# Reordering the first expert step of a hybrid SSD, Hyena and PEER backbone

## Chip, cores and metric

One core of one Trainium2 chip runs the whole program. The metric is the device time in microseconds from launch to end; lower is better. "Step", "turn" and "expert k" below are the program's own units and are explained with the kernel.

## The reference

A backbone of two layers works on 256 latent tokens of width 1024 (with 256 context tokens that only the first mixer reads). Layer 0 mixes tokens with a bidirectional Mamba-2 scan, layer 1 with an order-2 Hyena operator; after each mixer comes a PEER block. All arithmetic is float32. Per layer:

```python
x = layer_norm(DEEPNORM_ALPHA * x + g1 * y_lat, ln_g[i, 0], ln_b[i, 0])
x = layer_norm(DEEPNORM_ALPHA * x + g2 * peer_ffn(x * (1 + sc2) + sh2, *peer_w), ln_g[i, 1], ln_b[i, 1])
```

and the PEER block, cut to what matters:

```python
q = (t @ wq).reshape(T, PEER_HEADS, PEER_DK)                 # 8 heads, 256 wide
s1 = einsum('thd,hkd->thk', q[..., :half], k1)               # 128 keys per half
s2 = einsum('thd,hkd->thk', q[..., half:], k2)
v1, i1 = top_k(s1, 16); v2, i2 = top_k(s2, 16)
top_s, pos = top_k(v1[..., :, None] + v2[..., None, :], 16)  # 16 experts of 128*128
gate = softmax(top_s)
act = gelu(einsum('td,thkd->thk', t, u_tab[idx]))
out = einsum('thk,thkd->td', gate * act, v_tab[idx])
```

The Hyena filters are `sin` networks of 64 hidden features at 256 lags times a weight `h_f_w3` (64 by 2 orders, 2 sides, 1024 channels), with decay and a norm over the lags, taken to the frequency domain.

## The kernel before

**Tiles and steps.** The 256 tokens are two tiles of 128 (tile 0, tile 1). `peer(l)` runs the PEER block of layer l in 16 steps: step s is head s % 8 of tile s // 8. A step has 16 experts per token, k = 0 to 15, taken two at a time in a turn (`PAIR`). I number the experts of a layer through: expert 0 to 15 are step 0, expert 16 is the first of step 1.

**One expert's way.** POOL issues an indirect DMA (`pool.indirect_dma_start`, L1288) that gathers for each token its expert's two rows, 8 KB to each of 128 partitions, 1 MiB, into one of 8 slots (`uv`). DVE makes the dot product of the first row with the token (L2222), ACT the GELU of the turn's two dots (L1509), DVE multiplies by the gate (`weigh_experts`, L2154), ACT scales an identity to a diagonal (`diagonals`, L1517), and PE multiplies the second row by the diagonal into the output sum (`combine`, L1056), which frees the slot for the gather of the expert 8 later. For layer 0, slots 0 to 5 hold output weights of the mixer first: gather n of the first six waits for `out_weights_used` to reach n + 2, which `mixer_out(1, k0, k1)` counts up once for each second k; gathers 6 and 7 wait for its last product.

**What stands between the experts.** Each engine's order is written out by hand. On DVE, `choose(s, piece)` is the top-k of a later step in 8 pieces (0 to 3 the four top-8 searches of the two halves, 4 the candidate sums, 5 the top 16 of 256, 6 and 7 positions and expert numbers), placed in the turns between the dots and `weigh_experts`. The first step's choice, `choose_first`, stands ahead of all turns, as does `gates_of(0)`, which waits for ACT's `gate_exp(0)`. PE makes the queries of head s + 2 in four chunks of 8 products (`queries`, L1032) and their scores (L1043) in step s; ACT copies both out of PSUM (L1303) between its diagonals, in its own order, so a copy holds back the GELU behind it. Both heads 0 and 1 are handled ahead of the steps for tile 0 (`first_queries` L973, `second_queries` L999, `second_scores` L1009), woven into the mixer's output product of tile 1 (`mixer_out`, L934). Tile 1's own first norm, `second_tile` (`ln_stats`, `ln_norm`, `modulate_tile`: L1988 to L2027 and L1701), is done on DVE inside step 0, with PE's `tile_transposes(0, 1)` (L962) in the middle. The names of the turns in step 0 that place these pieces are the conditions `k == ...` of the listing.

**The filters.** In steps 8 to 15 of layer 0 the Hyena filters are made in four pieces (`filter_products` L1080 on PE, `filter_sides` and others on DVE). SP loads each piece's weights `w3` (`filter_piece`, L703): two DMAs, one for each side, each to 64 partitions, 128 KB each.

```python
w3 = early[0:HY_FF, 0:4, :].rearrange("p (s r) c -> p s r c", s=2)
hidden = dotj[0:HY_FF, 0:T]
```

The functions that the change touches follow.

## Time and profile before

| | |
|---|---|
| median of 3 runs | 1937.98 us (1936.33 to 1944.38) |
| profiled execution, its own time | 1935.79 us |
| its span, first to last instruction | 1934.0 us |
| granted TensorE clock, mean | 0.971 |
| busy: PE, DVE, ACT, POOL | 1690.3, 1500.2, 593.4, 483.3 us |
| HBM read | 662.79 MB, 343 GB/s over the span |
| gathers of expert rows | 512, 536.90 MB |
| layer 0's first gather issued, last part of its steps | 408.19 us, some 1088 us |

A page of the profile gives busy times by engine, the span in 40 slices, the DMA queues, the chain of work that ended last, and the costliest groups. The trace behind it gives each engine's instructions in order of time: start in us from the span's start, length, engine, line, operation, output <- inputs by the program's names, shapes, number merged, and in brackets the idle time ahead and what ended it. PE's rows count each float32 product several times (a `combine` is 4 rows, a k of `mixer_out` is 4).

### The profile page before, as it was taken

What the parts mean: (1) busy time and instruction counts of PE and PEld (TensorE: products, weight loads), DVE (VectorE), ACT (ScalarE), POOL (GpSimd) and SP (SyncE); (2) the same over time, 40 slices, a digit from 0 to 9 for tenths busy, and PEclk for the clock granted to TensorE, in tenths of its full rate; (3) what the DMA queues carried; (4) which work ended last, traced back from release to release, by engine and by line L of the source; (5) the groups of instructions that cost most, each with busy time, mean ns of one, the idle gap of its engine ahead of it and who ended that gap; (6) DMA issues with size and microseconds to landing.
All of it is one profiled execution on the core that took longest, in us unless ns stands there. A gap on an engine that the chain in (4) does not pass through costs nothing.

```text
span 1934.0 us, 18185 instructions
## 1 busy us (share of the span) xinstructions
PE 1690.3 (87%) x5422; PEld 934.6 (48%) x5422; DVE 1500.2 (78%) x3548; ACT 593.4 (31%) x1427; POOL 483.3 (25%) x516
## 2 busy tenths in 40 slices
PE   5999999997999877899898999879989987877776
PEld 5778468653554432343343677545444433332232
DVE  6899996766778767888886699787678778777755
ACT  2555672312222323323242121023222232322221
POOL 0000000022334333343333100023333333333331
PEclk9999999998999998998999999889999999999999
DMA  8333118978999999999999775679999999999996
GB/s 348 120 120 113 50 58 316 387 276 347 364 427 419 426 408 406 380 418 413 425 414 426 312 302 201 245 294 415 427 426 426 421 425 414 417 426 420 426 417 280
DMA packets 95170, 665.11 MB, mean 344 GB/s; under 512 B 11323, under 2 KB 13020, under 8 KB 15456
## 3 DMA queue, kind: packets, MB, share of 16 engines
q0 software_dynamic: 73728, 536.90, 67.3%
q1 hardware_dynamic: 21344, 127.05, 17.0%
q8 instruction: 43, 0.70, 0.1%
q14 instruction: 55, 0.45, 0.1%
HBM read 662.79 MB, written 1.11 MB: 343 GB/s over the span
## 4 chain that ended last, share of the span: by engine, by line
PE 47%; DMA 24%; DVE 20%; issue 4%; ACT 2%; PEld 1%; DVEq 0%; PEldq 0%; POOL 0%; SPq 0%; POOLq 0%; ACTq 0%
DMA expert_rows<-in_p_uv,chosen_experts 23%; PE bank L1056 23%; DVE dot_products L2222 4%; PE bank L1032 4%; PE bank L818 3%; PE bank L862 3%; PE bank L934 2%; DVE conv_work_or_state L1860 2%; DVE silu_c_row_and_products L1668 2%; PE bank L878 1%; PE bank L889 1%; PE bank L1248 1%; PE bank L1092 1%; ACT weight_diagonal L1517 1%; PE bank L1175 1%
## 5 line engine op out<-in xcount | busy, mean ns | idle before, releaser
L1056 PE MATMUL bank<-expert_rows,weight_diagonal 128*128 128x512 f32 x2048 | 967.8, 617 | 173.5 <-ACT weight_diagonal L1517 172.8
L1288 POOL DMA_INDIRECT expert_rows<-in_p_uv,chosen_experts x512 | 483.1, 944 | 1424.3 <-PE bank L1056 795.1
L2222 DVE SCALAR_TENSOR_TENSOR dot_products<-expert_rows,bank 128x1024 f32<-128x1024 f32 x512 | 624.9, 1220 | 255.6 <-DMA expert_rows<-in_p_uv,chosen_experts 241.6
L1056 PEld LDWEIGHTS bank<-expert_rows,weight_diagonal 128*128 128x128 f32 x2048 | 385.2, 196 | 689.1 <-issue 398.0
L1517 ACT ACTIVATE weight_diagonal<-constants,expert_weights 128x128 f32<-128x128 f32 x512 | 177.8, 394 | 243.8 <-DVE expert_weights L2154 235.3
L1509 ACT ACTIVATE expert_gelu<-expert_dots 128x2 f32<-128x2 f32 x258 | 52.3, 203 | 627.4 <-DVE dot_products L2222 627.0
L818 PE MATMUL bank<-mixer_input_T_hi,weights_hi 128*128 128x512 f32 (+1 forms) x192 | 74.8, 389 | 22.0 <-DVE mixer_input_T_lo L1752 14.7
L1860 DVE SCALAR_TENSOR_TENSOR conv_work_or_state<-conv_work_or_state,channel_vectors 128x252 f32<-128x252 f32 (+1 forms) x192 | 82.5, 431 | 4.9 <-ACT conv_work_or_state L1371 0.4
L1175 PE MATMUL bank<-hyena_input_T,hyena_weight_block 128*128 128x256 f32 x320 | 71.1, 380 | 4.3 <-DMA hyena_weight_block<-in_h_in_blocks 4.3
L818 PE MATMUL bank<-mixer_input_T_lo,weights_hi 128*128 128x512 f32 (+1 forms) x192 | 72.4, 377 | 0.0
L818 PE MATMUL bank<-mixer_input_T_hi,weights_lo 128*128 128x512 f32 (+1 forms) x192 | 72.4, 377 | 0.0
L1175 PEld LDWEIGHTS bank<-hyena_input_T,hyena_weight_block 128*128 128x128 f32 x320 | 60.2, 190 | 14.8 <-DMA hyena_weight_block<-in_h_in_blocks 5.6
L2154 DVE TENSOR_TENSOR expert_weights<-expert_gelu,expert_gates 128x2 f32<-128x2 f32 x258 | 41.8, 162 | 30.7 <-ACT expert_gelu L1509 22.8
L1668 DVE SCALAR_TENSOR_TENSOR silu_c_row_and_products<-weight_block,silu_c_row_and_products 128x1024 f32<-128x1024 f32 x48 | 58.6, 1222 | 2.4
L862 PE MATMUL bank<-weight_block,mixer_input_T 128*128 128x256 f32 x256 | 58.5, 382 | 0.0
L1032 PE MATMUL bank<-t_T,weight_block 128*128 128x256 f32 x224 | 53.2, 380 | 0.0
L818 PEld LDWEIGHTS bank<-mixer_input_T_hi,weights_hi 128*128 128x128 f32 x192 | 37.1, 193 | 30.8 <-issue 14.8
L1032 PEld LDWEIGHTS bank<-t_T,weight_block 128*128 128x128 f32 x224 | 42.9, 192 | 18.4 <-issue 14.0
L862 PEld LDWEIGHTS bank<-weight_block,mixer_input_T 128*128 128x128 f32 x256 | 47.6, 190 | 7.5 <-issue 1.6
L1509 ACT ACT_TABLE_LOAD x38 | 48.8, 1283 | 0.7
L934 PE MATMUL bank<-out_weights,output_input_T 128*128 128x512 f32 x96 | 42.2, 592 | 0.0
L2222 DVE DVE_READ_ACCUMULATOR dot_products<-expert_rows,bank 128x1 f32 x512 | 42.2, 82 | 0.0
(298 smaller groups left out, 1935.8 us busy)
## 6 DMA issues: line engine op xcount, KB each, us to landing
weight_block<-in_ada_rows SPq DMA_DIRECT2D x24, 1024.0 KB, 7.0
weight_block<-in_m_in_blocks SPq DMA_DIRECT2D x20, 1024.0 KB, 4.9
hyena_weight_block<-in_ada_rows SPq DMA_DIRECT2D x16, 1024.0 KB, 5.4
hyena_weight_block<-in_h_in_blocks SPq DMA_DIRECT2D x12, 1024.0 KB, 7.3
weight_block<-in_wq_blocks SPq DMA_DIRECT2D x11, 1024.0 KB, 7.6
expert_rows<-in_p_uv,chosen_experts POOLq DMA_INDIRECT x512
out_weights<-in_m_out_blocks SPq DMA_DIRECT2D x6, 1024.0 KB, 9.5
hyena_weight_block<-in_h_out_blocks SPq DMA_DIRECT2D x4, 1024.0 KB, 7.2
```

What stands on the lines that cost most here:

```text
L818: last = mm(ps[b][:, c0:2 * T], lhs[q % 2][:, k, :], rhs[:, k, c0:2 * T], start=(k + n == 0), stop=(k == KD - 1 and n == 2))
L862: last = mm(ps[b][:, t * BLK:(t + 1) * BLK], hT[:, k, T + t * P:T + (t + 1) * P], w[:, k * BLK:(k + 1) * BLK], start=(k == 0), stop=(k == ...
L934: last = mm(ps[b][:, :], uT[:, t, k, :], out_w[k // 2][:, k % 2, h * 512:(h + 1) * 512], start=(k == 0), stop=(k == INNER // P - 1))
L1032: last = mm(ps[b][:, c * T:(c + 1) * T], wk[:, c * P:(c + 1) * P], tT[:, k, :], start=(k == 0), stop=(k == KD - 1))
L1056: last = mm(ps[b][:, :], dg[n % DIAG][:, :], uv[slot][:, D + h * 512:D + (h + 1) * 512], start=(r == 0 and k == 0), stop=end)
L1175: last = mm(ps[b][:, c * T:(c + 1) * T], w[:, k * BLK + c * P:k * BLK + (c + 1) * P], hhT[:, k, :], start=(k == 0), stop=(k == KD - 1))
L1288: pool.indirect_dma_start(uv[slot][:, :], None, A[f"p_uv{l}"], bass.IndirectOffsetOnAxis(ap=chosen[:, s_, k:k + 1], axis=0)).then_inc(uv_l ...
L1509: f(gel[:, s_, k:k + width], dots[:, s_, k:k + width], ACT.Gelu).then_inc(sem("gelu_done"), 1)
L1517: f(dg[n % DIAG][:, :], ident, ACT.Copy, scale=ew[:, s_, k:k + 1]).then_inc(sem("diagonal_ready"), 1)
L1668: stt(dotj[:, :], weights_, 1.0, c_rows[row], ALU.mult, ALU.mult, accum_out=o[:, m // KD, m % KD:m % KD + 1]).then_inc(sem("modulation_row ...
L1860: last = stt(o, s_, conv_tap(q, i, j), o, ALU.mult, ALU.add)
L2222: stt(prod[:, :], uv[slot][:, 0:D], 1.0, rows_t, ALU.mult, ALU.mult, accum_out=dots[:, s_, k + j:k + j + 1]).then_inc(sem("dots_done"), 1)
```

## The change

Six things change, all in layer 0, and five of them ahead of or inside step 0:

- PE ahead of the steps: `token_rows(0, 0)` and three of `mixer_out(1, ...)`'s k (5 to 7) stand ahead of the second head's queries; two more k (8, 9) stand between its queries and its scores, and six behind.
- PE, step 0: tile 1's transposes stand ahead of expert 2 (were ahead of expert 6). Head 2's query chunks come at k = 4, 6, 8, 10 (were 8, 10, 12, 14), its scores at k = 12 (were 15).
- DVE, step 0: `second_tile` follows the turn of experts 2 and 3 (was 4 and 5). The choice for step 1 starts in the first turn: pieces 0, 1; then 2, 3; then 4; then 5; then 6, 7 (were pairs in turns 1 to 4).
- ACT, step 0: `ln_root` at k = 2 (was 4); head 2's queries are copied at k = 10, its scores at k = 12 (both were at 14).
- SP: a filter piece's weights are one DMA of 256 KB to 128 partitions, side 0 on partitions 0 to 63 and side 1 on 64 to 127, from a table that the host lays out in that order; the hidden features are loaded twice (64 KB each), once for each half of the partitions.
- PE's filter products of side 1 then read partitions 64 to 127.

Layer 1's conditions give the same turns as before.

```diff
-    w3 = early[0:HY_FF, 0:4, :].rearrange("p (s r) c -> p s r c", s=2)
+    w3 = early[:, 0:2, :]
...
-    hidden = dotj[0:HY_FF, 0:T]
+    hidden = dotj[:, 0:T]
...
         wait_full(sp, ("q", 0, HALVED))
-        sp.dma_start(hidden, hdram).then_inc(sem("filter_in"), 16)
+        for side in range(2):
+            sp.dma_start(hidden[side * HY_FF:(side + 1) * HY_FF, :], hdram).then_inc(sem("filter_in"), 16)
...
-            c = A["h_f_w3"][0][:, o * 2 * D:(o + 1) * 2 * D].rearrange("p (s c) -> p s c", s=2)
-            for side in range(2):
-                sp.dma_start(w3[:, side, :, :], halves(c[:, side, h * 512:(h + 1) * 512])).then_inc(sem("filter_weights_in"), 16)
+            sp.dma_start(w3, halves(A["filter_weights"][m])).then_inc(sem("filter_weights_in"), 16)
...
-                        pe.wait_ge(sem("filter_weights_in"), 32 * (m + 1))
-                        pe.wait_ge(sem("filter_in"), 32)
+                        pe.wait_ge(sem("filter_weights_in"), 16 * (m + 1))
+                        pe.wait_ge(sem("filter_in"), 48)
                     for side in range(2):
                         b = begin(("hflt", m, t, side))
-                        mm(ps[b][:, :], hidden[:, t * P:(t + 1) * P], w3[:, side, :, :], start=True, stop=True).then_inc(full[b], 1)
+                        f = slice(side * HY_FF, (side + 1) * HY_FF)
+                        mm(ps[b][:, :], hidden[f, t * P:(t + 1) * P], w3[f, :, :], start=True, stop=True).then_inc(full[b], 1)
...
-                    if l == 0 and s_ == 0 and k == 6:
+                    if l == 0 and s_ == 0 and k == 2:
                         tile_transposes(0, 1)
...
-                    chunks = ((8, 10, 12, 14), (2, 5, 8, 11))[l] if s_ == 0 else (0, 1, 2, 3)
+                    chunks = ((4, 6, 8, 10), (2, 5, 8, 11))[l] if s_ == 0 else (0, 1, 2, 3)
...
-                    if r < PH and k == min(chunks[-1] + 2, TOPK - 1):
+                    if r < PH and k == chunks[-1] + 2:
                         scores(r)
...
         first_half_scores(0, 1)
+        token_rows(0, 0)
+        mixer_out(1, 5, 8)
         for c in range(2):
             second_queries(0, 0, c, 0, KD)
-        mixer_out(1, 5, 6)
+        mixer_out(1, 8, 10)
         second_scores(0, 0)
-        token_rows(0, 0)
-        mixer_out(1, 6, INNER // P)
+        mixer_out(1, 10, INNER // P)
         peer(0)
...
-                    if l == 0 and s_ == 0 and k == 4:
+                    if l == 0 and s_ == 0 and k == 2:
                         ln_root(0, 0, 1)
-                    if s_ + 2 < PH and k == (14 - 2 * l if s_ == 0 else 4):
+                    if s_ + 2 < PH and k == (10 + 2 * l if s_ == 0 else 4):
                         copy_queries(s_ + 2)
-                    if s_ + 2 < PH and k == (14 if s_ == 0 else 6):
+                    if s_ + 2 < PH and k == (12 + 2 * l if s_ == 0 else 6):
                         copy_scores(s_ + 2)
...
-                    if s_ == 0 and 1 <= n < 5:
+                    if l == 0 and s_ == 0 and n < 5:
+                        for piece in ((0, 1), (2, 3), (4,), (5,), (6, 7))[n]:
+                            choose(1, piece)
+                    elif l and s_ == 0 and 1 <= n < 5:
                         for piece in range(2):
                             choose(1, 2 * (n - 1) + piece)
...
-                    if l == 0 and s_ == 0 and k == 4:
+                    if l == 0 and s_ == 0 and k == 2:
                         second_tile()
```

Two places show what this does to an engine's order. The first is PE from the first head's last score to expert 2, 3 or 8: `mixer_out` (its weights `out_weights`), the second head's queries (`weight_block`) and scores (`keys_T`), `token_rows` (`constants,t_T`), the experts (`expert_rows`), tile 1's transposes (`constants,x_residual`). Before:

```order
L984 MATMUL bank<-keys_T,q_T 128x128
L999 MATMUL bank<-t_T,weight_block 128x128 x16
L934 MATMUL bank<-out_weights,output_input_T 128x512 x2
L1009 MATMUL bank<-keys_T,q_T 128x128 x2
L1017 MATMUL bank<-constants,t_T 128x128 x8
L934 MATMUL bank<-out_weights,output_input_T 128x512 x20
L1056 MATMUL bank<-expert_rows,weight_diagonal 128x512 x12
L962 MATMUL bank<-constants,x_residual 128x128 x8
L1056 MATMUL bank<-expert_rows,weight_diagonal 128x512 x6
```

and changed (line numbers are one lower):

```order
L983 MATMUL bank<-keys_T,q_T 128x128
L1016 MATMUL bank<-constants,t_T 128x128 x8
L933 MATMUL bank<-out_weights,output_input_T 128x512 x6
L998 MATMUL bank<-t_T,weight_block 128x128 x16
L933 MATMUL bank<-out_weights,output_input_T 128x512 x4
L1008 MATMUL bank<-keys_T,q_T 128x128 x2
L933 MATMUL bank<-out_weights,output_input_T 128x512 x12
L1055 MATMUL bank<-expert_rows,weight_diagonal 128x512 x4
L961 MATMUL bank<-constants,x_residual 128x128 x8
L1055 MATMUL bank<-expert_rows,weight_diagonal 128x512 x6
```

Three k of the mixer's product moved ahead of the second head's queries and two more ahead of its scores, and only two experts instead of six stand ahead of the transposes.

The second is ACT in step 0, from the exponentials of step 1's gates (`gate_exponentials`, between two table loads) to the diagonals of experts 14 and 15. Before:

```order
L1504 ACT_TABLE_LOAD
L1504 ACTIVATE gate_exponentials,gate_sums<-selected_scores 128x16
L1509 ACT_TABLE_LOAD
L1509 ACTIVATE expert_gelu<-expert_dots 128x2
L1517 ACTIVATE weight_diagonal<-constants,expert_weights 128x128 x2
L1509 ACTIVATE expert_gelu<-expert_dots 128x2
L1517 ACTIVATE weight_diagonal<-constants,expert_weights 128x128 x2
L1303 ACTIVATE q_T<-bank 128x512
L1303 ACTIVATE scores<-bank 128x512
L1509 ACTIVATE expert_gelu<-expert_dots 128x2
L1517 ACTIVATE weight_diagonal<-constants,expert_weights 128x128 x2
```

and changed, from the GELU of experts 8 and 9 on:

```order
L1510 ACTIVATE expert_gelu<-expert_dots 128x2
L1518 ACTIVATE weight_diagonal<-constants,expert_weights 128x128 x2
L1510 ACTIVATE expert_gelu<-expert_dots 128x2
L1518 ACTIVATE weight_diagonal<-constants,expert_weights 128x128 x2
L1304 ACTIVATE q_T<-bank 128x512
L1505 ACT_TABLE_LOAD
L1505 ACTIVATE gate_exponentials,gate_sums<-selected_scores 128x16
L1510 ACT_TABLE_LOAD
L1510 ACTIVATE expert_gelu<-expert_dots 128x2
L1518 ACTIVATE weight_diagonal<-constants,expert_weights 128x128 x2
L1304 ACTIVATE scores<-bank 128x512
L1510 ACTIVATE expert_gelu<-expert_dots 128x2
L1518 ACTIVATE weight_diagonal<-constants,expert_weights 128x128 x2
```

The copy of head 2's queries (`q_T`) now stands ahead of the gates' exponentials and their two table loads, and the GELU of experts 12 and 13 behind them; the copy of the scores moved ahead of the GELU of experts 14 and 15.

## Rows read from the trace of the kernel before

**Rows 1.** The page, section 2: the span in 40 slices of 48.35 us

```profile
GB/s 348 120 120 113 50 58 316 387 276 347 364 427 419 426 408 406 380 418 413 425 414 426 312 302 201 245 294 415 427 426 426 421 425 414 417 426 420 426 417 280
```

**Rows 2.** Windows; engines' busy us, then clock, DMA share, GB/s

```profile
440.00:454.00 14.00, 5.81 (x13) 2.36 (x11) 13.41 (x39) 1.39 (x5) 0.94 (x1) 0.63 0.71 300
532.00:580.00 48.00, 44.66 (x152) 26.09 (x151) 34.59 (x87) 12.31 (x36) 15.92 (x17) 0.96 1.01 427
```

**Rows 3.** Timeline of PE, 402 to 482 us; start, length, engine, line, idle ahead

```profile
402.23 3.81 PE L999 MATMUL bank<-t_T,weight_block 128*128 128x128 f32 x32 [0.46 <-ACT scores L1303]
...
408.91 17.33 PE L934 MATMUL bank<-out_weights,output_input_T 128*128 128x512 f32 x40
426.08 7.03 PE L1056 MATMUL bank<-expert_rows,weight_diagonal 128*128 128x512 f32 x16
...
439.37 1.09 PE L962 MATMUL bank<-constants,x_residual 128*128 128x128 f32 x8 [1.42 <-DVE x_residual L2027]
448.65 7.50 PE L1056 MATMUL bank<-expert_rows,weight_diagonal 128*128 128x512 f32 x12 [8.19 <-ACT weight_diagonal L1517]
455.99 1.89 PE L1032 MATMUL bank<-t_T,weight_block 128*128 128x256 f32 x8
457.71 3.60 PE L1056 MATMUL bank<-expert_rows,weight_diagonal 128*128 128x512 f32 x8
461.15 1.89 PE L1032 MATMUL bank<-t_T,weight_block 128*128 128x256 f32 x8
...
474.91 1.05 PE L1043 MATMUL bank<-keys_T,q_T 128*128 128x128 f32 x8
479.24 3.43 PE L1056 MATMUL bank<-expert_rows,weight_diagonal 128*128 128x512 f32 x4 [3.27 <-ACT weight_diagonal L1517]
```

**Rows 4.** Timeline of DVE, 402 to 477 us

```profile
414.03 1.22 DVE L2222 SCALAR_TENSOR_TENSOR dot_products<-expert_rows,bank 128x1024 f32<-128x1024 f32 x1 [2.47 <-DMA expert_rows<-in_p_uv,chosen_experts]
...
424.40 1.22 DVE L2222 SCALAR_TENSOR_TENSOR dot_products<-expert_rows,bank 128x1024 f32<-128x1024 f32 x1 [2.79 <-DMA expert_rows<-in_p_uv,chosen_experts]
...
427.50 0.16 DVE L2154 TENSOR_TENSOR expert_weights<-expert_gelu,expert_gates 128x2 f32<-128x2 f32 x1
...
431.00 1.22 DVE L2222 SCALAR_TENSOR_TENSOR dot_products<-expert_rows,bank 128x1024 f32<-128x1024 f32 x1 [2.19 <-DMA expert_rows<-in_p_uv,chosen_experts]
...
433.60 0.16 DVE L2154 TENSOR_TENSOR expert_weights<-expert_gelu,expert_gates 128x2 f32<-128x2 f32 x1
...
442.62 1.21 DVE L2222 SCALAR_TENSOR_TENSOR dot_products<-expert_rows,bank 128x1024 f32<-128x1024 f32 x1
...
445.63 0.43 DVE L2063 MAX8 selected_scores<-candidates 128x8 f32<-128x256 f32 x1
...
448.00 0.16 DVE L2154 TENSOR_TENSOR expert_weights<-expert_gelu,expert_gates 128x2 f32<-128x2 f32 x1
...
453.52 0.16 DVE L2154 TENSOR_TENSOR expert_weights<-expert_gelu,expert_gates 128x2 f32<-128x2 f32 x1
...
476.63 0.29 DVE L2063 MAX8 top_values<-scores 128x8 f32<-128x128 f32 x1 [7.30 <-ACT scores L1303]
```

**Rows 5.** Timeline of ACT, 402 to 477 us

```profile
408.24 0.39 ACT L1303 ACTIVATE scores<-bank 128x256 f32<-128x256 f32 x1 [1.78 <-PE bank L1009]
...
457.34 1.28 ACT L1504 ACT_TABLE_LOAD   x1
...
460.26 0.20 ACT L1509 ACTIVATE expert_gelu<-expert_dots 128x2 f32<-128x2 f32 x1
```

**Rows 6.** Timeline of POOL, 423 to 453 us

```profile
423.08 0.94 POOL L1288 DMA_INDIRECT expert_rows<-in_p_uv,chosen_experts  x1 [2.50 <-PE bank L934]
...
452.71 0.94 POOL L1288 DMA_INDIRECT expert_rows<-in_p_uv,chosen_experts  x1 [13.27 <-PE bank L1056]
```

**Rows 7.** Windows, as rows 2: after the filter weights' first load

```profile
704.00:738.00 34.00, 26.32 (x50) 10.16 (x49) 21.48 (x60) 9.33 (x24) 10.21 (x12) 0.86 1.02 385
```

**Rows 8.** Timeline of PE, a restart in the fourth step

```profile
570.52 2.56 PE L1056 MATMUL bank<-expert_rows,weight_diagonal 128*128 128x512 f32 x4 [2.05 <-ACT weight_diagonal L1517]
```

2 lines of the change are left out of this document (added).

## Prediction

> **What bounds the kernel now.** I read the page's slices first, then windows, then the engines' timelines over the first expert step.
>
> In the slices the expert steps of layer 0 run from slice 9 on. The gathers move 427 GB/s in slice 12 and about that in most that follow, but 276, 347 and 364 in slices 9 to 11, 387 to 532 us [rows 1]. In the window 532 to 580 us the DMA engines' share is 1.01 at 427 GB/s while PE, DVE and ACT are each idle at times: there the queue is the limit, and at that rate a gather of 1.05 MB takes 2.46 us. From 440 to 454 us the share is 0.71, and PE is busy 5.81 of 14 us at a clock of 0.63 [rows 2]. So time can be won only ahead of the point at which the queue fills, about expert 30, and what is won there should shift everything behind it: all later work of layer 0 hangs on gathers and their slots.
>
> PE's timeline names two holes: 8.19 us ahead of expert 6 (448.65) and 3.27 ahead of expert 16 (479.24), each followed by rows at half rate: 3.43 us for expert 16's four products, where two experts in a row take 3.44 (457.71 to 461.15) [rows 3]. The first hole is the second tile's norm on DVE. It begins after 433.60, and the next dot starts at 442.62; then come two dots and two pieces of choice before 448.00. The second is DVE waiting 7.30 us for head 2's scores, which PE makes only after expert 15 [rows 3, 4]. POOL waits 13.27 us for a slot behind the first hole [rows 6].
>
> **The change part by part.** All durations are differences of starts in the rows. Two dots take 2.48 us, pieces 0 and 1 of a choice 1.95 (424.40 + 1.15 to 427.50), pieces 2 and 3 1.45 (431.00 + 1.15 to 433.60), piece 4 0.54 and piece 5 2.37 (442.62 + 2.47 to 445.63 to 448.00), pieces 6 and 7 2.96 (448.08 + 2.48 to 453.52), the tile's norm 8.94 (433.68 to 442.62), its transposes starting 5.7 into it [rows 3, 4]. From `weigh_experts` to PE it is 0.65 (448.00 to 448.65). An expert or a query chunk on PE is 1.72, a k of the mixer 1.72 (17.33 for ten) [rows 3].
>
> *PE ahead of the steps.* PE's wait of 0.46 us for the copy of a score goes, since other work stands there [rows 3]; the rest is only reordered. Expert 0 starts at 425.8 instead of 426.08. The second head's scores end near 401.8 + 0.9 + 5.2 + 3.7 + 3.4 + 0.4 = 415.4; they stood ahead of 408.24 [rows 5]. ACT's `gate_exp(0)` is behind their copy, and DVE's first dot behind its gates: copy 0.4, a table load 1.28, 0.36 for the exponentials [rows 5], 0.5 for the gates. The first dot moves from 414.03 to about 418. This added wait is hidden: expert 0's weights are then ready at 418.1 + 2.5 + 1.95 + 0.65 = 423.2, and PE comes at 425.8. With 2.6 us less cover it would count in full. Gathers 2 to 5 are issued 0.5 to 2 us earlier; a gather lands 7.9 us after its issue (423.08 to 431.00) [rows 4, 6], so expert 3 is there by 423.3, in time.
>
> *DVE and the tile's norm.* Dots and pieces 2, 3 end at 422.6 + 2.48 + 1.45 = 426.6. The norm starts there, 7.1 us earlier, since the choice of step 1 no longer stands behind idle dots. PE has done experts 0 and 1 at 429.2, waits 3.1 us for the transposes (432.3), and finishes experts 2 and 3 by 437. DVE is free at 435.5; two dots, piece 4, and expert 4 starts on PE at 435.5 + 2.48 + 0.54 + 0.65 = 439.2, after a hole of 2.2.
>
> *PE from expert 4 on.* Eight experts and four chunks are 12 × 1.72 = 20.6: 459.9. DVE just keeps up: expert 6 is ready at 444.2 for PE's 444.4, expert 8 at 449.7 for 449.6.
>
> *ACT in between.* The copy of head 2's queries waits for the fourth chunk at 458.2 and takes 0.6; behind it now stand two table loads and an exponential, 2.92 from the first load to the next GELU (457.34 to 460.26) [rows 5]. So experts 12 and 13 get their GELU at 461.7 and PE at 462.6. This is a new hole of 2.7 us, where before the same loads were hidden.
>
> *Head 2's scores.* PE makes them at 464.4. Before, DVE could resume its choice 1.72 after their start (474.91 to 476.63) [rows 3, 4]; now the copy is done by 466.1. Step 1's gates (0.5), two dots and pieces 0 and 1 follow: 471.0, and expert 16 starts at 471.6 instead of 479.24, 7.6 us earlier. The hole ahead of it is about 1.2 us and should not slow the clock: 1.42 did not (439.37, eight short products in 1.09) [rows 3]. So its own 1.7 us at half rate go too: 9.3 us at expert 17. From there PE runs step 1 without a hole, as it did, and the queue fills at the same distance.
>
> *The clock.* Holes of 8.19, 3.27 and 2.05 us were each followed by rows near half rate, the last with 2.56 us for an expert [rows 3, 8]. The new order has holes of 3.1, 2.2 and 2.7. A slow stretch behind the first two is largely eaten by the wait for DVE; one behind the third delays head 2's scores and costs 1.7 us. Its bounds are 0 and 3.4 (two holes). I take 1.7, as for expert 16, since 2.05 was enough once.
>
> *The filters.* The bytes are the same: 256 KB a piece. PE has half-height products as before and waits for no load that the rows show. After the first piece the gathers ran at 385 GB/s for 34 us at full share [rows 7], against 427: 34 × (1 − 385/427) = 3.3 us lost. Nothing ties this to the form of the load, so the likeliest is 0, bounded by 3.3 gained and 3.3 more lost for each other piece. The Trainium skill's page "DMA: Bandwidth & Descriptors", "Why a DMA increments its semaphore by 16 and not by 1", says that 64 partitions already use all 16 engines; by that rule the wider load has nothing to win. No row here shows the engines apart. The second load of the hidden features (64 KB, 0.15 us of the queue) is nothing.
>
> The sum is 9.3 − 1.7 = 7.6 us. The profiled execution took 1935.79 and would take 1928.2; it lies 2.2 below the median of 1937.98, from which I get 1930.4. 0.5%, 9.7 us, is about what a measurement can tell from no change.
>
> **The rivals.**
>
> *The clock stays up* through the 2.7 us hole, as it did through 1.42: 9.3 us, 1928.7. For it: whether a hole slows PE is not certain between 1.4 and 2.05. Against: one of 2.05 us, shorter than this, was enough [rows 8].
>
> *The filter loads were the cause* of the slow 34 us: 3.3 more, with the clock as forecast 10.9, 1927.1. For it: they began right ahead [rows 7]. Against: the bytes are few, and the stretch outlasts them.
>
> *A table switch costs more.* A switch of ACT's tables could drain the engine too. Here that would have to show between the first load and the GELU, and it is 2.92 us for two switches [rows 5], 1.28 of load each. If each cost 1.4 more, the new hole would be 5.5 and the gain 4.8: 1933.2. The Trainium skill, "ScalarE: Activation LUTs", "What ACT_TABLE_LOAD costs", states 2.66 us for a switch, load and drain. The trace disagrees, so little is left for it.
>
> *The win is given back.* If in steps 8 to 15 something not tied to the gathers set the pace, the shift would shrink there: 0 to 2 us left, 1937. I see no such wait.
>
> *Slower.* The new load writes all 128 partitions from one block of memory. If each of the four pieces is followed by a stretch as in rows 7 where only the first was, 3 × 3.3 = 9.9 us are lost against 7.6 won: 1940.3. It decides from 2.3 such stretches on. Only the first piece shows a long one, so this is weak.
>
> **How the numbers follow.** Forecast 0.46, clock up 0.21, filters 0.12, table switch 0.04, given back 0.10, slower 0.07. The likeliest gives 1930.4. The range goes from both gains together (9.3 + 3.3, 1925.4) to nearly nothing won, 1937. Faster by over 0.5% means below 1928.3: half of "clock up", most of "filters", a twelfth of the forecast, 0.27. Slower by over 0.5% is 0.03, a part of the last case. The rest, 0.70, is within.
>
> **What would show it.** Right: the norm's first instruction on DVE near 426.6, transposes near 432.3, expert 4 on PE near 439.2, a hole of about 2.7 us ahead of expert 12 ended by a diagonal, expert 16 near 472 to 473, no wait of DVE for head 2's scores over 1 us, and the same 427 GB/s from gather 30 on. Wrong: the first dot later than 420.5 and PE waiting at expert 0; DVE late for experts 6 or 8; a shift at expert 17 that is not found again when layer 0's last gather lands; or filter pieces whose surroundings move other rates than before.

## The result, and the profile after

The changed kernel takes 1920.37 us (median of 11 runs, 1918.04 to 1927.52), the kernel before beside it 1937.69 (11 runs, 1930.08 to 1944.38): ratio 0.9933, 95% interval 0.9918 to 0.9948. Three more sets of runs of the same pair gave 0.9937, 0.9941 and 0.9939. So the change wins some 12 us (11 to 13), where 7.6 was forecast. The ratio of a set is not the quotient of its two medians, which is up to 0.002 away from it (0.9911 in the first set); where they differ I go by the ratio. The four sets' medians of the changed kernel are 1920.4 to 1922.5, those of the kernel before 1932.4 to 1937.7.

The changed kernel's profiled execution took 1918.49 us (span 1916.7, clock 0.981), one of its fastest, against 1935.79 before. Its slices:

```profile
GB/s 351 111 131 112 44 67 294 388 291 378 392 426 425 427 426 394 405 416 425 426 418 427 281 295 237 242 299 422 427 427 427 426 425 418 419 427 425 417 421 275
```

Slices 9 to 11 hold 291, 378 and 392 GB/s where [rows 1] has 276, 347 and 364: the queue fills earlier. Windows of the changed kernel; the columns are those of [rows 2]:

```profile
440.00:454.00 14.00, 14.00 (x46) 8.31 (x45) 12.94 (x35) 2.69 (x9) 5.17 (x5) 1.00 0.95 349
532.00:580.00 48.00, 45.84 (x155) 25.46 (x153) 35.95 (x96) 12.95 (x38) 17.53 (x19) 1.00 1.01 424
696.00:730.00 34.00, 26.06 (x57) 10.04 (x56) 24.23 (x65) 9.54 (x25) 12.84 (x14) 1.00 1.02 427
```

PE is busy 14.00 of 14 us where it was 5.81, at full clock. The last row is the surprise: behind the first filter piece the gathers now move 427 GB/s, where [rows 7] has 385.

PE's timeline of the changed kernel over step 0, which answers to [rows 3]:

```profile
421.83 3.17 PE L933 MATMUL bank<-out_weights,output_input_T 128*128 128x512 f32 x7
424.83 3.60 PE L1055 MATMUL bank<-expert_rows,weight_diagonal 128*128 128x512 f32 x8
431.54 1.09 PE L961 MATMUL bank<-constants,x_residual 128*128 128x128 f32 x8 [3.11 <-DVE x_residual L2028]
432.47 3.60 PE L1055 MATMUL bank<-expert_rows,weight_diagonal 128*128 128x512 f32 x8
438.45 1.98 PE L1055 MATMUL bank<-expert_rows,weight_diagonal 128*128 128x512 f32 x4 [2.38 <-ACT weight_diagonal L1518]
440.27 1.89 PE L1031 MATMUL bank<-t_T,weight_block 128*128 128x256 f32 x8
...
457.60 1.88 PE L1055 MATMUL bank<-expert_rows,weight_diagonal 128*128 128x512 f32 x4
462.29 1.99 PE L1055 MATMUL bank<-expert_rows,weight_diagonal 128*128 128x512 f32 x4 [2.82 <-ACT weight_diagonal L1518]
464.11 1.05 PE L1042 MATMUL bank<-keys_T,q_T 128*128 128x128 f32 x8
465.00 5.32 PE L1055 MATMUL bank<-expert_rows,weight_diagonal 128*128 128x512 f32 x12
471.54 1.98 PE L1055 MATMUL bank<-expert_rows,weight_diagonal 128*128 128x512 f32 x4 [1.22 <-ACT weight_diagonal L1518]
```

There are four holes (3.11, 2.38, 2.82, 1.22), and in this execution an expert takes 1.98 us or two take 3.60 behind every one: full rate. ACT in the third hole:

```profile
457.88 0.60 ACT L1304 ACTIVATE q_T<-bank 128x512 f32<-128x512 f32 x1 [5.84 <-PE bank L1031]
458.49 1.28 ACT L1505 ACT_TABLE_LOAD   x1
...
460.11 1.28 ACT L1510 ACT_TABLE_LOAD   x1
461.41 0.20 ACT L1510 ACTIVATE expert_gelu<-expert_dots 128x2 f32<-128x2 f32 x1
```

The loads stand behind the copy, 2.92 us from the first to the GELU as in [rows 5]: the new hole is there, for the reason and at the length that were forecast.

POOL's rows of gathers 104 and 255 (before, then changed), which frame steps 6 to 15 of layer 0:

```profile
684.70 0.94 POOL L1288 DMA_INDIRECT expert_rows<-in_p_uv,chosen_experts  x1 [2.05 <-PE bank L1056]
...
1075.39 0.94 POOL L1288 DMA_INDIRECT expert_rows<-in_p_uv,chosen_experts  x1 [0.78 <-PE bank L1056]
```

```profile
675.65 0.94 POOL L1289 DMA_INDIRECT expert_rows<-in_p_uv,chosen_experts  x1 [2.07 <-PE bank L1055]
...
1060.56 0.94 POOL L1289 DMA_INDIRECT expert_rows<-in_p_uv,chosen_experts  x1 [0.78 <-PE bank L1055]
```

At gather 104 the changed kernel is 9.05 us ahead, at gather 255 it is 14.83. So a second gain of 5.8 us arises between them, in steps whose order the change doesn't touch: there only the filters differ. (Of the six changes listed ahead of the prediction two, the filters' load and their products, act there, so four and not five belong to step 0 and what stands ahead of it.) Behind gather 255, where the code is the same in both, the lead grows by 2.5 more in this pair of executions; in the three other profiles of the changed kernel it changes by -3.3, -0.4 and +1.7.

The filter products are where PE differs. Before (first fence) and changed (second), one pair of sides:

```profile
776.46 1.98 PE L1080 MATMUL bank<-scores,silu_c_row_and_products 64*128 64x512 f32 x4
778.37 2.84 PE L1056 MATMUL bank<-expert_rows,weight_diagonal 128*128 128x512 f32 x6
```

```profile
765.25 1.13 PE L1080 MATMUL bank<-scores,silu_c_row_and_products 64*128 64x512 f32 x4
766.31 3.27 PE L1055 MATMUL bank<-expert_rows,weight_diagonal 128*128 128x512 f32 x7
```

From its start to the next expert the pair takes 1.91 us before and 1.06 now: side 1 on the upper 64 rows of the array runs beside side 0 on the lower. The Trainium skill, "TensorE: Matmul & The Clock Gate", "Part 3: Packing small matmuls — row/col tiling", says that products on different row groups run concurrently in one array; the trace agrees. There are 8 such pairs, so at most 8 × 0.85 = 6.8 us of PE; two of the eight take longer here, 1.40 and 1.54 us. What that is worth at the end is another question, which the experiments take up.

### The profile page after: what moved, and what is told of

The parts are those of the page before. It is cut to its first block, busy times and chain, and to the rows that moved or that the text cites. A ratio compares the mean times of both kernels' runs of the same rounds, so it can differ in the third digit from the quotient of the medians.

```text
span 1916.7 us, 18183 instructions
## 1 busy us (share of the span) xinstructions
PE 1671.8 (87%) x5422; PEld 924.0 (48%) x5422; DVE 1499.4 (78%) x3548; ACT 593.6 (31%) x1427; POOL 483.0 (25%) x516
## 4 chain that ended last, share of the span: by engine, by line
PE 43%; DMA 25%; DVE 23%; issue 4%; ACT 2%; PEld 1%; DVEq 0%; PEldq 0%; POOL 0%; SPq 0%; POOLq 0%; ACTq 0%
DMA expert_rows<-in_p_uv,chosen_experts 24%; PE bank L1055 20%; DVE dot_products L2223 6%; PE bank L1031 3%; PE bank L817 3%; PE bank L861 3%; PE bank L933 2%; DVE conv_work_or_state L1861 2%; DVE silu_c_row_and_products L1669 2%; PE bank L877 1%; PE bank L888 1%; PE bank L1249 1%; ACT weight_diagonal L1518 1%; PE bank L1176 1%; DMA hyena_weight_block<-in_h_in_blocks 1%
## 5 line engine op out<-in xcount | busy, mean ns | idle before, releaser
L1055 PEld LDWEIGHTS bank<-expert_rows,weight_diagonal 128*128 128x128 f32 x2048 | 380.1, 193 | 685.6 <-issue 388.2
```

The costliest lines, as they stand in the source:

```text
L1055: last = mm(ps[b][:, :], dg[n % DIAG][:, :], uv[slot][:, D + h * 512:D + (h + 1) * 512], start=(r == 0 and k == 0), stop=end)
```

## The experiments

Each was timed beside the kernel before on one chip. Two spans of the profile, read from POOL's rows as above, separate the two gains: gathers 8 to 24 (step 0 and the start of step 1), and gathers 104 to 255. All eighteen, and the two first profiles ("64" and "128" are the partitions that one load writes):

| run | 8 to 24, us | 104 to 255, us | median, us | ratio to before, interval |
|---|---|---|---|---|
| before, first profile | 53.94 | 390.7 | 1937.69 | 1 |
| e4, before | 53.55 | 390.7 | 1934.47 | 1.0008 (0.9994 to 1.0023) |
| changed, first profile | 46.05 | 384.9 | 1920.37 | 0.9933 (0.9918 to 0.9948) |
| e3, changed | 46.05 | 383.5 | 1922.47 | 0.9937 (0.9924 to 0.9951) |
| e16, changed | 46.53 | 383.8 | 1921.74 | 0.9941 (0.9922 to 0.9960) |
| e18, changed | 46.53 | 382.2 | 1921.75 | 0.9939 (0.9922 to 0.9956) |
| e1, order alone | 46.06 | 394.3 | 1928.50 | 0.9965 (0.9952 to 0.9978) |
| e2, filters alone | 54.45 | 382.6 | 1930.74 | 0.9983 (0.9970 to 0.9997) |
| e5, products apart | 46.52 | 388.2 | 1927.29 | 0.9943 (0.9924 to 0.9962) |
| e17, the same | 46.52 | 386.0 | 1926.50 | 0.9965 (0.9948 to 0.9981) |
| e6, two loads of 64, old table | 46.07 | 400.3 | 1928.27 | 0.9956 (0.9940 to 0.9973) |
| e7, two loads of 64, one half | 46.52 | 396.0 | 1926.81 | 0.9960 (0.9939 to 0.9982) |
| e10, one load of 64 | 46.54 | 389.9 | 1927.47 | 0.9976 (0.9958 to 0.9994) |
| e9, two loads of 128 | 46.53 | 383.1 | 1922.75 | 0.9945 (0.9927 to 0.9962) |
| e11, scores late | 50.25 | 382.9 | 1925.50 | 0.9948 (0.9925 to 0.9970) |
| e12, the same kernel | 50.27 | 383.4 | 1924.86 | 0.9955 (0.9937 to 0.9973) |
| e13, norm and scores late | 51.56 | 382.1 | 1926.37 | 0.9956 (0.9937 to 0.9975) |
| e14, longer hole | 46.35 | 386.9 | 1921.95 | 0.9936 (0.9918 to 0.9954) |
| e8, exponentials first | 44.91 | 382.8 | 1919.74 | 0.9915 (0.9898 to 0.9932) |
| e15, the same | 44.91 | 382.7 | 1920.03 | 0.9938 (0.9914 to 0.9961) |

### The two halves of the change

**Order alone** (the six filter lines of the diff undone):

> The whole reordering of the first expert step, the filters' weights, load and products as before. The trace of the change showed expert 17 9.4 us earlier and no fall of the granted clock. Theory A (the order gives 9.4 us, and the filters give the rest): 9 to 10 us under the kernel before, ratio about 0.995; the shift of the gathers stands at 9 to 9.5 us from expert 24 to the end of layer 0, and two sides' products of a filter tile start one after the other, 0.43 us apart, 1.9 to 2.0 us for the pair. Theory B (the order gives all of the difference, because PE and the queue keep gaining behind step 1): 12 to 14 us under, ratio about 0.993. Theory C (the forecast's clock term was right and the profiled run an exception): 7 to 8 us under, ratio 0.996, with a stretch at half rate behind the hole ahead of expert 12.

Ratio 0.9965, 6.8 us. Step 0 is that of the changed kernel to 0.01 us, and the lead at gather 104 is 9.25 us. Behind it the gain is partly lost: two stretches of slow gathers, one after the first and one after the fourth filter piece. So Theory A holds for the order's own part up to gather 104; less of it arrives at the end than the 9 to 10 us it named. Theory B falls, and Theory C's slow stretch at expert 12 isn't there.

**Filters alone** (from the diff; PE's waits, the hidden features and the products follow as in the change):

```diff
-    w3 = early[0:HY_FF, 0:4, :].rearrange("p (s r) c -> p s r c", s=2)
+    w3 = early[:, 0:2, :]
...
-            for side in range(2):
-                sp.dma_start(w3[:, side, :, :], halves(c[:, side, h * 512:(h + 1) * 512])).then_inc(sem("filter_weights_in"), 16)
+            sp.dma_start(w3, halves(A["filter_weights"][m])).then_inc(sem("filter_weights_in"), 16)
```

> The filters alone: weights and hidden features on all partitions, one load a piece, products of side 0 and side 1 on the lower and upper rows; the order as before. Theory A (the two sides' products run side by side on PE, and each pair gives back about 0.85 us): 2 to 5 us under the kernel before; the pair's products start within 0.05 us of each other. Its largest amount is 8 pairs by 0.85 = 6.8 us, less what the gathers' queue hides. Theory B (nothing in it, since the queue sets the pace there): within 1 us of the kernel before, though the products still run side by side. Theory D (the old load made the slow stretch behind the first piece): the gathers behind 698 us run at 427 GB/s in place of 385, 3.3 us under.

Ratio 0.9983, 3.3 us. Gathers 104 to 255 take 382.6 instead of 390.7 us, 8.1 less. This profile began 2.4 us late at gather 0, in code that is the same in both, so its end hides a part of that.

> The changed kernel once more, beside the others on one chip: 10 to 16 us under the kernel before. The sum of the two parts alone (order, filters) is to come to this one within 1.5 us if they don't depend on each other; if the filters only pay once the order has moved, it is more than the sum by 2 us or more.

Ratio 0.9937, 12.2 us against 6.8 + 3.3 = 10.1 for the parts. That is 2.1 apart, more than the 1.5 expected but less than the uncertainty of each, about 2.5 us either way; whether the parts help each other stays open.

> The kernel before, unchanged, as a control: ratio 1.000 within 0.002. Its profile is to show what differs from one execution to the next: if the 34 us at 385 GB/s behind the first filter piece (704 to 738 us) belong to the kernel they are there again within a few us of the same place; if they are a passing disturbance of the transfers they are gone or elsewhere, and the time that the gathers lose in layer 1 differs from the first profile's by 1 to 3 us too.

Ratio 1.0008. The slow stretch behind the first piece is there again: 379 GB/s from 700 to 738. It belongs to the kernel. The same windows, with the columns of [rows 2], in three kernels: before again, e10 (64 partitions in one load), and e18 (changed).

```profile
660.00:690.00 30.00, 24.77 (x68) 11.17 (x67) 21.07 (x58) 8.74 (x23) 12.19 (x13) 1.00 1.01 426
700.00:738.00 38.00, 29.25 (x57) 11.00 (x57) 24.24 (x68) 10.23 (x27) 12.20 (x13) 0.91 1.02 379
```

```profile
660.00:690.00 30.00, 23.56 (x58) 9.65 (x56) 21.56 (x56) 8.19 (x22) 12.05 (x13) 1.00 1.01 427
700.00:738.00 38.00, 30.23 (x58) 11.85 (x57) 24.38 (x66) 9.14 (x26) 12.25 (x14) 0.87 1.01 392
```

```profile
660.00:690.00 30.00, 24.71 (x58) 10.43 (x57) 21.82 (x59) 8.26 (x22) 11.97 (x13) 0.94 1.01 426
700.00:738.00 38.00, 30.72 (x64) 11.91 (x63) 27.10 (x71) 10.35 (x28) 14.10 (x15) 0.96 1.01 426
```

### What in the load makes the slow stretches

The last packets of SP's loads for a piece start 9 to 17 us after the issue, but the slow rate goes on for 20 us and more behind them, with no packet of SP's queue. Two loads became one, 64 partitions 128, the table contiguous. Four kernels separate these.

**Two loads of 64 from the old table, to both halves**, the rest as changed:

```diff
-            sp.dma_start(w3, halves(A["filter_weights"][m])).then_inc(sem("filter_weights_in"), 16)
+            for side in range(2):
+                sp.dma_start(w3[side * HY_FF:(side + 1) * HY_FF, :, :], halves(c[:, side, h * 512:(h + 1) * 512])).then_inc(sem("filter_weights_in"), 16)
```

> The changed kernel with the products side by side, but each piece fetched as before from the old table, by two loads of 64 rows 16 KB apart, each to its own half of the partitions. Stretches in which a gather's 8 KB packets take 342 in place of 309 ns, for 20 to 50 us on end, followed 4 of the 12 pieces in the three profiles with the old load and none of the 12 in the three with the new. If the old table's rows or the two loads cause them: they come back behind one or two of the four pieces, 3 to 6 us over the changed kernel. If the old place of the load (one half of the partitions) caused them: none, within 1 us of the changed kernel.

Slow from the third piece on until beyond the fourth:

```profile
872.00:950.00 78.00, 64.02 (x144) 25.99 (x144) 59.23 (x144) 24.81 (x59) 26.21 (x28) 1.00 1.02 376
960.00:1010.00 50.00, 43.62 (x101) 18.37 (x100) 40.79 (x99) 16.23 (x38) 16.74 (x18) 1.00 1.01 385
```

The place on one half isn't needed for the stretches.

**Two loads of 64 from the new table, to one half**, products one after the other (the diff is against the kernel with the order alone, e1):

```diff
-                sp.dma_start(w3[:, side, :, :], halves(c[:, side, h * 512:(h + 1) * 512])).then_inc(sem("filter_weights_in"), 16)
+                sp.dma_start(w3[:, side, :, :], halves(A["filter_weights"][m][side * HY_FF:(side + 1) * HY_FF, :])).then_inc(sem("filter_weights_in"), 16)
```

> The order of the changed kernel, filters on one half of the partitions and products one after the other as before, but fetched from the new contiguous table by two loads of 64 rows. The counterpart of the run with two loads. If the place on one half causes the slow stretches: they are there, ratio as for the order alone, 0.9965. If the old table's rows cause them: none, and 3 to 4 us under the order alone, 0.9945.

Slow behind the fourth piece, 387 GB/s from 960 to 1010. So it isn't the old table's rows either. What is left is the number of loads or their 64 partitions.

**Two loads of 128**, else as changed:

```diff
-            sp.dma_start(w3, halves(A["filter_weights"][m])).then_inc(sem("filter_weights_in"), 16)
+            for r in range(2):
+                sp.dma_start(w3[:, r, :], A["filter_weights"][m][:, r * 256:(r + 1) * 256]).then_inc(sem("filter_weights_in"), 16)
```

> The changed kernel, each filter piece fetched in two loads of 128 partitions by 1 KB each in place of one of 128 by 2 KB. So far slow stretches (8 KB packets of the gathers at 342 to 352 ns for 20 us and more) stand behind 7 of the 20 pieces of the five profiles with two loads of 64 partitions, whatever the table and the place, and behind none of the 20 of the five profiles with one load of 128. If it is the number of loads: they come back behind one or two of the four pieces, 3 to 6 us over the changed kernel, and the single times spread over more than 8 us. If it is the 64 partitions: none, within 1 us of the changed kernel, times within 6 us.

None, and its five times lie within 2.6 us.

**One load of 64** by 4 KB, with the new order and products one after the other (again against e1; the table is laid out anew, in 64 rows of 4 KB):

```diff
-            for side in range(2):
-                sp.dma_start(w3[:, side, :, :], halves(c[:, side, h * 512:(h + 1) * 512])).then_inc(sem("filter_weights_in"), 16)
+            sp.dma_start(early[0:HY_FF, 0:4, :], A["filter_weights"][m].rearrange("p (r c) -> p r c", r=4)).then_inc(sem("filter_weights_in"), 16)
```

> The order of the changed kernel, filters on one half of the partitions and products one after the other as before, but each piece in one load of 64 partitions by 4 KB. If it is the number of loads that makes the slow stretches: none, times within 6 us of each other, ratio 0.994 (about as the run with the products apart). If it is the 64 partitions: they are there, times spread over 8 us and more, ratio 0.996.

The stretch is there behind the first piece (the second of the three fences of windows above), and its twelve times reach from 1923 to 1942 us. It is the 64 partitions, not the number of loads nor the table nor the half. Over all profiles, each of the six kernels or repeats with loads on 64 partitions has at least one slow stretch behind a piece (8 of 24 pieces, 36 to 146 us long), and none of the fourteen with loads on 128 has one.

The packets show it more plainly than the long stretches, which look like chance. Take the median time of the gathers' 8 KB packets in steps of 2 us, from 4 to 10 us after a piece's load is issued: behind each of the 24 pieces with loads on 64 partitions it reaches 348 to 394 ns, from 309 ahead of the load (but for e6's fourth piece, where the stretch of the third was still on), and behind none of the 56 with loads on 128 does it leave 309. So every such load slows the gathers for some 4 to 6 us, and in 8 of 24 cases they stay slow. Windows behind the second piece, e10 (64) and e18 (128):

```profile
792.00:796.00 4.00, 1.98 (x5) 0.57 (x3) 3.85 (x11) 0.20 (x1) 1.87 (x2) 1.00 1.04 365
```

```profile
790.00:794.00 4.00, 1.14 (x4) 0.31 (x3) 3.78 (x14) 0.80 (x3) 1.43 (x2) 1.00 1.03 424
```

Why the gathers stay slow behind a load that is over is open. One run of e15 took 1942.38 us with loads on 128, so this isn't the only thing that makes a long run.

### The products side by side

```diff
-                if not second and k in (1, 8):
+                if not second and k in (1, 2, 8, 9):
...
-                    for side in range(2):
+                    for side in (k - 1 - 7 * t,):
```

> The changed kernel, but the second side's product of a filter tile is issued one expert later than the first side's, so the two can't run side by side; the load is the new one. In the profiles so far the kernels with both filter edits gained 5.8 to 8.1 us more against the kernel before between gathers 104 and 255 than those without. If what counts is the products side by side (Theory A): 3 to 5 us over the changed kernel (ratio to before 0.996), with no slow stretch behind a filter piece. If what counts is the load (Theory D): within 1 us of the changed kernel, 0.9935.

> The changed kernel with the two sides' filter products one expert apart, again, now beside the changed kernel on one chip. Between gathers 104 and 255 the first profile of it won 2.5 us on the profile of the kernel before, and eleven with products side by side and loads on all partitions won 3.8 to 8.6, 7 in the middle. If the products side by side carry it: again 2 to 4 us there, and 2.5 to 5 us over the changed kernel at the end. If the first run was an exception: 6 to 8 us there, and within 1 us of the changed kernel.

> The changed kernel beside it: ratio to before 0.9935 within 0.0015; 6 to 8 us won between gathers 104 and 255, no slow stretch behind a filter piece.

In the second profile of the products apart (e17) a side stands alone, 1.05 us to the next expert, and again for side 1:

```profile
769.64 1.12 PE L1080 MATMUL bank<-scores,silu_c_row_and_products 64*128 64x512 f32 x2
770.69 1.98 PE L1055 MATMUL bank<-expert_rows,weight_diagonal 128*128 128x512 f32 x4
772.60 1.12 PE L1080 MATMUL bank<-scores,silu_c_row_and_products 64*128 64x512 f32 x2
773.66 2.84 PE L1055 MATMUL bank<-expert_rows,weight_diagonal 128*128 128x512 f32 x6
```

Gathers 104 to 255 take 388.2 and 386.0 us, against 382.1 to 386.9 (middle 383) in the twelve profiles with both filter edits; e18's 382.2 is 8.5 less than before, a little over the 6 to 8 expected. No slow stretch. On one chip it is 1926.50 against 1921.75 for the changed kernel, 4.8 us, and no time of the one lies within those of the other (1923.5 to 1932.1 against 1920.2 to 1922.6). The first ratio (0.9943) alone would have said nothing. So taking the products apart costs 3 to 5 us.

That is not yet what the change won over the old form. Apart, a pair costs PE 2 × 1.05 us where the old form took 1.91, and side 1 reaches DVE 2.9 us later; neither was separated. Two other readings give less. e6 and e7, side by side on one chip, both fetch by two loads of 64 partitions, and the one has the products side by side and the other one after the other: ratios 0.9956 and 0.9960, less than 1 us, with some 5 us of uncertainty (the medians, 1928.27 and 1926.81, even go the other way). And the packets give an estimate of the load's part. Between gathers 104 and 255 the gathers' packets of 325 to 500 ns take, over 309 ns each and divided by the 16 engines, 5.7 and 7.6 us in the two profiles of the kernel before, 6.3 to 17.8 in the four others with loads of 64, and 0.5 to 1.3 in the fourteen with loads of 128. Without that time the five profiles with the old products come to 383 to 385 us and e6 to 382.5, and the twelve with both filter edits to 381 to 386 (middle 382). So of the 8 us in steps 6 to 15 the load has 5 to 7, and 1 to 3 are left for the products side by side. What they are worth at the end is somewhere from 0 to 5 us and stays open.

### How the order's gain divides, and the clock

**Scores late:** chunks at experts 8, 10, 12, 14, scores behind 15, copies at 14, as before.

```diff
-                    chunks = ((4, 6, 8, 10), (2, 5, 8, 11))[l] if s_ == 0 else (0, 1, 2, 3)
+                    chunks = ((8, 10, 12, 14), (2, 5, 8, 11))[l] if s_ == 0 else (0, 1, 2, 3)
...
-                    if r < PH and k == chunks[-1] + 2:
+                    if r < PH and k == min(chunks[-1] + 2, TOPK - 1):
```

ACT's conditions for the two copies go back likewise.

> The changed kernel with head 2's query chunks at experts 8, 10, 12, 14, its scores behind expert 15 and its copies on ACT in the turn of expert 14, as before; the norm stays early. PE then has no hole ahead of expert 12 (the table loads are hidden again) and one of 2.6 + 1.7 - 1.3 = 3.0 us ahead of expert 16: start of expert 4 (438.5) + 12 experts and 4 chunks (27.5) + 4.3 = 470.3 for expert 16, against 471.5. So moving the scores was worth nothing by itself: within 1 us of the changed kernel if the clock stays up behind a hole of 3.0 us, 1.7 us over it if it falls as in the profile of the kernel before.

Gathers 8 to 24 take 50.25 us, 3.7 to 4.2 more than in the changed kernel, where 0 or 1.7 were expected. What the expectation left out: without chunks between them experts 6 and 8 wait for DVE's weights. PE's rows:

```profile
445.62 3.70 PE L1055 MATMUL bank<-expert_rows,weight_diagonal 128*128 128x512 f32 x8 [1.22 <-ACT weight_diagonal L1518]
451.13 1.98 PE L1055 MATMUL bank<-expert_rows,weight_diagonal 128*128 128x512 f32 x4 [1.81 <-ACT weight_diagonal L1518]
...
476.20 3.29 PE L1055 MATMUL bank<-expert_rows,weight_diagonal 128*128 128x512 f32 x4 [3.27 <-ACT weight_diagonal L1518]
```

The early chunks fill PE's time where DVE sets the pace, and the hole ahead of expert 16 comes back at 3.27 us, here with a slow expert behind it.

**The same kernel again.** The expectation below speaks of a kernel with the norm late too, but the one that ran was e11's, so it says nothing on the norm. As a repeat of e11 it agrees: 50.27 us, the hole of 3.27, and 3.78 behind it.

> As the run with the scores late, and tile 1's norm, its root and its transposes back in their old turns too (the choice of step 1 and the work ahead of the steps stay as changed). Expert 6 starts at about 446 (before 448.7, changed kernel 441.9), expert 16 at 446 + 10 experts and 4 chunks (24.1) + 4.3 = 474.4: 2.9 us over the changed kernel if the clock stays up, 4.6 to 6.3 us over if it falls behind the hole of 7 to 8 us ahead of expert 6, or behind both.

**Norm and scores late**, which adds to e11:

```diff
-                    if l == 0 and s_ == 0 and k == 2:
+                    if l == 0 and s_ == 0 and k == 6:
                         tile_transposes(0, 1)
...
-                    if l == 0 and s_ == 0 and k == 2:
+                    if l == 0 and s_ == 0 and k == 4:
                         second_tile()
...
-                    if l == 0 and s_ == 0 and k == 2:
+                    if l == 0 and s_ == 0 and k == 4:
                         ln_root(0, 0, 1)
```

> The kernel that the run named both late was meant to be: tile 1's norm, root and transposes and head 2's chunks, scores and copies in their old turns, all else as changed. Expert 6 starts 3 to 4.5 us later than in the changed kernel (441.9), expert 16 behind it by 14 x 1.72 + 4.3. If the early norm is what carries the gain: 2 to 4 us over the run with the scores late alone. If PE's continuous block (experts 6 to 15 and the chunks) makes up for it: within 1 us of it. The hole of 7 to 8 us ahead of expert 6 is followed by half rate, as in three of three profiles before.

51.56 us, 1.3 more than e11; the medians (1926.37 against 1925.50 and 1924.86) lie between the two expectations and tell neither from the other. The hole ahead of expert 6 is 7.65 us, and the three experts behind it take 8.29 us where three at full rate take 5.3: a good part of it at half rate, as expected.

This gives the parts between gathers 8 and 24, at like clock at expert 16 (e11 has 1.7 us of slow rows there, 3.29 + 2.32 against 1.98 + 1.89, so 48.5 without them): e4 53.6, with PE's new order ahead of the steps and the choice over five turns 51.6, with the early norm 48.5, with the early scores 46.1 to 46.5. So 2, 3 and 2 us, each from one or two profiles. The early scores without the early norm can't be had, since their chunks need tile 1's transposes.

In e13 (first fence) the hole of 3.27 us ahead of expert 16 left PE at full rate, as in e4 (second):

```profile
479.19 1.98 PE L1055 MATMUL bank<-expert_rows,weight_diagonal 128*128 128x512 f32 x4 [3.27 <-ACT weight_diagonal L1518]
```

```profile
480.07 1.98 PE L1056 MATMUL bank<-expert_rows,weight_diagonal 128*128 128x512 f32 x4 [3.27 <-ACT weight_diagonal L1517]
```

That makes six profiles with a hole of 3.27 us there: four with 3.29 to 3.78 us behind it ([rows 3] among them), two with 1.98.

**Longer hole**, three small copies more on ACT ahead of the copy of head 2's queries (they write where nothing reads):

```diff
+                if l == 0 and r == 2:
+                    b = wait_full(act, ("q", l, r))
+                    for i in range(3):
+                        f(pause[:, i, :], ps[b][:, 0:32], ACT.Copy)
                 copy_out(("q", l, r), qT[r % 2][:, :, :].rearrange("p a t -> p (a t)"))
```

> The changed kernel with three extra small copies on ACT ahead of the copy of head 2's queries (into a place that nothing reads), so that the hole ahead of expert 12 grows from 2.8 to 3.4 or 3.5 us. In the profiles so far nine holes of 2.82 us and thirteen of 1.2 us there left PE at full rate, and of five of 3.27 us ahead of expert 16 four were followed by an expert of 3.3 to 3.8 us in place of 1.98. If the length of the hole decides: expert 12 takes about 3.4 us, the time is 0.6 + 1.4 to 1.9 us over the changed kernel. If it is what the engine did long before, with the two long holes of the old order, that decides: 1.98 us, and 0.6 over.

The copies overlapped, and the hole grew to 3.09 us, not 3.4:

```profile
462.74 1.98 PE L1056 MATMUL bank<-expert_rows,weight_diagonal 128*128 128x512 f32 x4 [3.09 <-ACT weight_diagonal L1523]
```

Full rate, and a time like the changed kernel's. So it didn't reach the length in dispute, and the question behind it is not answered. (The expectation counts nine holes of 2.82 us by then; there were eight. With e16, e17 and e18 eleven profiles have it, each at full rate.)

### Without the new hole

```diff
+                    if l == 0 and s_ == 0 and k == 10:
+                        gate_exp(1)
                     if s_ + 2 < PH and k == (10 + 2 * l if s_ == 0 else 4):
                         copy_queries(s_ + 2)
...
-                    if s_ < PH and k == 10:
+                    if s_ < PH and k == 10 and (l or s_):
                         gate_exp(s_ + 1)
```

> The changed kernel with step 1's exponentials ahead of the copy of head 2's queries on ACT, in the turn of expert 10, so that the table loads no longer stand between that copy and the GELU of experts 12 and 13. The hole of 2.8 us ahead of expert 12 shrinks to 0 (both loads ahead of the copy) or to 1.5 (the load of the GELU's table stays behind it); head 2's scores and expert 16 come 1.3 to 2.8 us earlier, and as the queue fills later, the end does too: 1 to 3 us under the changed kernel, ratio to before 0.9925. If what is won there is eaten by DVE's dots or by a slot, expert 17 stands where it was, and the time too.

> The run with the exponentials first again, beside the changed kernel on one chip: expert 17 stood 1.6 us earlier than in the changed kernel, each against its own gather 8. If that arrives at the end: 1 to 2.5 us under the changed kernel; if it is eaten before the queue fills: the same within 0.5 us.

> The changed kernel once more, as the measure for the three others of this call: ratio to before 0.9935 within 0.0015, no slow stretch behind a filter piece, its times within 8 us of each other.

ACT in e8: the first load and the exponentials now stand in its idle time, and the GELU's load stays behind the copy.

```profile
454.53 1.28 ACT L1505 ACT_TABLE_LOAD   x1
...
460.35 0.60 ACT L1304 ACTIVATE q_T<-bank 128x512 f32<-128x512 f32 x1 [4.22 <-PE bank L1031]
460.96 1.28 ACT L1510 ACT_TABLE_LOAD   x1
462.26 0.20 ACT L1510 ACTIVATE expert_gelu<-expert_dots 128x2 f32<-128x2 f32 x1
```

The hole is 1.20 us, gathers 8 to 24 take 44.91 in both, 1.1 to 1.6 less than the changed kernel. On one chip the medians are 1920.03 and 1921.74. It is 1.7 us in the direction expected, but the intervals of the ratios overlap, so it is not shown at the end; in step 0, where two profiles agree to 0.01 us, it is.

## Why the prediction was wrong

**What held.** The walk through step 0, with the changed kernel's trace beside it:

| step | forecast | measured |
|---|---|---|
| expert 0 on PE | 425.8 | 424.83 |
| norm starts on DVE | 426.6 | 425.85 |
| transposes | 432.3 | 431.54 |
| expert 4 | 439.2 | 438.45 |
| hole ahead of expert 12, it starts | 2.7, 462.6 | 2.82, 462.29 |
| expert 16 | 471.6 | 471.54 |
| gain at expert 17 with the clock up | 9.3 | 9.4 |

The trace as a whole began 0.56 us earlier (gather 0), so most rows are right to a few tenths, and each hole was ended by what the forecast named. The gain kept its size to gather 104 (9.05), as "the queue fills at the same distance" said. The cost of the table switches was right.

**The step that failed first: the filters.** The sum gave them 0, and they brought 3.8 to 8.6 us between gathers 104 and 255, 8 in the middle, and, by the ratios, 3.3 us (filters alone) to 5.4 us (changed kernel less order alone) at the end. Two sentences stand for that 0. The first, "nothing ties this to the form of the load, so the likeliest is 0", was the larger miss: 64 partitions tie it, as e6, e7 and e10 against e9 show, and by the packets' times the old load costs the gathers 5 to 7 us in the kernel before, where one stretch of 3.3 us had been the bound. The rows did show a stretch right behind the load; what was missing was a second profile of the same kernel, which would have shown it again. The rival "the filter loads were the cause" had the mechanism with a chance of 0.12 and the amount of one stretch. The reason against it, that "the stretch outlasts them", was true and proved nothing. The second, "PE has half-height products as before", is wrong as it stands: on different rows of the array they run side by side, up to 0.85 us less for a pair. I read "as before" from the shape and not from the partitions, though the change's own words are that side 1 reads partitions 64 to 127. How much of that arrives at the end is open (0 to 5 us). The rule of the Trainium skill that the text weighed ("DMA: Bandwidth & Descriptors", "Why a DMA increments its semaphore by 16 and not by 1") was used for a gain in the load's own speed; no run shows the engines apart, and the loss wasn't in the load but in the gathers beside and behind it.

**The second: the clock.** Of 9.3 us 1.7 was taken off for a slow stretch behind the hole of 2.7, because 2.05 us had been enough once [rows 8]. It wasn't: 2.82 us slowed nothing in eleven of eleven profiles, while 3.27 did in four of six. Ahead of the row of 2.56 us behind 2.05 PE had been idle before as well: from 560 to 570 us of the kernel before it was busy 7.45 of 10 us. Whether that made the difference no run shows, but the length of a single hole was the wrong measure to carry over. For the hole of 2.8 us the rival "the clock stays up" was right.

**The sum by what the runs show:** at expert 17 the order gives 9.4 us against the first profile of before, where 9.3 was forecast, and 8.5 against the second, which had no slow expert behind its 3.27 us. So the 1.7 us of expert 16 at half rate, which the 9.3 hold, were won against one execution of the kernel before and not against the other: that 9.3 met 9.4 so closely is in part luck. The filters give 3.8 to 8.6 us more between gathers 104 and 255. The profiles of the changed kernel end 12.4 to 17.3 us ahead of the first of before, the medians of the runs 11 to 17, and the ratios say 11.4 to 13. What isn't settled is why the filters alone measured 3.3 us (0.6 to 5.8) where their profile has 8 in those steps, and the order alone 6.8 where its profile is 9.25 ahead at gather 104; the slow stretches, which fall differently in each execution, are a likely reason, but no run tests it.

**The range** ended at 1925.4, both gains together, 9.3 and one stretch of 3.3 us. That was too short, since the load's part was bounded by the one stretch seen in one profile and the products had no term. The starting value had a part in it too: the forecast of 1930.4 counts from 1937.98 us, and the sets of runs of the kernel before lie at 1932.4 to 1937.7.

## What to carry to other kernels

If a profile shows a shared queue at full share but below its usual rate, look at the last transfer that began before it, and try another shape of that transfer before calling it chance. Look at the time of single packets too: they showed the effect behind every load, where the long stretches came behind one in three. A wide spread of single times can be a sign of it (e10 19 us, e9 2.6), though not a sure one: e15, with loads on 128, spread over 27 us by one run. When an edit puts operands on other partitions, price it on PE too: two products of 64 rows took 1.06 us together, as long as one of them alone (1.05), when they lay on different rows of the array. And a product that PE has to make anyway is worth most where PE waits for another engine: the early chunks filled such time, which a sum of PE's own durations doesn't show.

## What the runs showed of the hardware

- A load of 256 KB onto 64 partitions by SP's queue, in one or two transfers, slowed the 8 KB packets of POOL's gathers from 309 ns to between 348 and 394 for some 4 to 6 us behind all 24 pieces seen, and behind 8 of them left the gathers at 376 to 393 GB/s for 36 to 146 us, in place of 427; the same bytes onto 128 partitions, in one load or two, did neither in fourteen profiles.
- Whether PE is slow behind a hole is in part a matter of the execution. The hole of 3.11 to 3.13 us ahead of the transposes is the same in every kernel with the early norm. Where it ended between 431.45 and 431.70 us (five profiles) the eight short products behind it took 1.09 us; where it ended between 432.00 and 433.88 (ten, e16 and e18 of the changed kernel among them) they ran at half rate, 1.97 us for eight. In e12 it ended at 430.87; the eight took 1.19 us, and the two experts behind them 5.24 in place of 3.60. The slow stretch was largely eaten by the wait for DVE, as forecast for this hole: gathers 8 to 24 took 46.5 us with it and 46.1 without.
